# A 512-token block: other tokens on the 128 partitions, and its loads and stores cut into four pieces

## What is computed

```python
mod = (silu(c) @ w_ada + b_ada)                      # shift, scale, gate for both sub-layers
h = rmsnorm(x, norm1_g) * (1 + sc1) + sh1
u_in, gate_c, gate_b, q, k, v, g_conv, g_attn = split_projection(h @ w_in)
conv_y = short_conv(gate_c * u_in, conv_w, past)     # causal, width 3: needs tokens t-1 and t-2
y_conv = (gate_b * conv_y) @ w_conv_out
q, k = rope_partial(q, pos), rope_partial(k, pos)
attn_o = dilated_mixture(q, k, v)                    # 3 head groups, (window, dilation) = (128,1), (512,4), (2048,16)
mixed = (sigmoid(g_conv) * y_conv + sigmoid(g_attn) * (attn_o @ w_attn_out)) @ w_o
x = x + gt1 * mixed
x = x + gt2 * hier_moe(rmsnorm(x, norm2_g) * (1 + sc2) + sh2, ...)   # 16 experts, two per token
y = rmsnorm(x, normf_g)
# outputs: y, the keys and values of the prompt (k1_p ... v3_p; of group 1 only the last 128 tokens),
# the last two rows of the convolution's input, and the caches of the sampled sequences moved on by 4 rows
```

## Time and profile before

| | |
|---|---|
| median of three executions | 1200.55 us (1200.52 to 1203.01) |
| profiled execution: its own time | 1200.55 us |
| profiled execution: span from the first to the last instruction | 1198.5 us |
| PE busy | 94% of the span |
| DVE, ACT, POOL busy | 46%, 30%, 16% |
| mean granted clock of TensorE | 0.979 of full speed |
| bytes moved by DMA | 350.36 MB, mean 292 GB/s |

### The profile page before, as it was taken

One profiled execution on the slowest core, in us unless ns is written; L12 is line 12 of the kernel. 1 busy time (PEld: TensorE's weight loads), 2 busy tenths in 40 slices (PEclk: granted clock), 3 DMA queues, 4 the chain that ended last, 5 costly groups with the idle time before them and its releaser, 6 DMA issues.

```text
span 1198.5 us, 28853 instructions
## 1 busy us (share of the span) xinstructions
PE 1123.4 (94%) x12074; PEld 966.8 (81%) x12074; DVE 549.1 (46%) x1215; ACT 358.7 (30%) x655; POOL 187.0 (16%) x257
## 2 busy tenths in 40 slices
PE   4898999999999999999989999999969899999987
PEld 3797999999999998987769999999526567777762
DVE  1744565656565644543254444345723323322327
ACT  5422333333333323331054444432501101110103
POOL 0332233233330100000000000000050111111130
PEclk9998999999999999999979999999979999999998
DMA  9999978978756597748798788287729999999964
GB/s 351 387 342 374 328 253 296 315 240 284 279 185 219 184 376 270 264 158 298 269 335 301 264 290 297 88 275 294 287 75 356 376 411 419 408 403 409 420 170 143
DMA packets 167729, 350.36 MB, mean 292 GB/s; under 512 B 14670, under 2 KB 119326, under 8 KB 153105
## 3 DMA queue, kind: packets, MB, share of 16 engines
q1 hardware_dynamic: 151825, 324.91, 74.0%
q0 software_dynamic: 6272, 16.09, 4.4%
q10 hardware_dynamic: 9552, 8.21, 2.1%
HBM read 322.06 MB, written 115.20 MB: 365 GB/s over the span
## 4 chain that ended last, share of the span: by engine, by line
PE 85%; DVE 5%; DMA 4%; issue 3%; ACT 2%; SPq 1%; DVEq 0%; ACTq 0%
PE psum L927 44%; PE psum L1277 16%; PE psum L1289 7%; PE psum L1002 3%; PE psum L988 2%; PE psum L977 2%; PE psum L968 2%; PE psum L871 2%; PE psum L1024 2%; DMA kvr<-in_cache_v_dram 1%; DMA wraw<-in_w_in_dram 1%; DMA adar<-in_w_ada_dram 1%; PE psum L1051 1%; PE psum L1310 1%; PE psum L948 1%
## 5 line engine op out<-in xcount | busy, mean ns | idle before, releaser
L927 PE MATMUL psum<-hHi,whi 128*128 128x272 f32 x1216 | 359.0, 295 | 2.8 <-DVE hLo L1694 1.9
L927 PE MATMUL psum<-hLo,whi 128*128 128x272 f32 x1216 | 351.5, 289 | 0.0
L927 PE MATMUL psum<-hHi,wlo 128*128 128x272 f32 x1216 | 349.9, 288 | 0.0
L927 PEld LDWEIGHTS psum<-hHi,whi 128*128 128x128 f32 x1216 | 229.3, 189 | 15.6 <-issue 10.0
L927 PEld LDWEIGHTS psum<-hHi,wlo 128*128 128x128 f32 x1216 | 229.4, 189 | 0.0
L927 PEld LDWEIGHTS psum<-hLo,whi 128*128 128x128 f32 x1216 | 228.7, 188 | 0.0
L1277 PE MATMUL psum<-e,xs 128*32 128x256 f32 x3072 | 199.2, 384 | 22.3 <-issue 19.3
L1277 PEld LDWEIGHTS psum<-e,xs 128*32 128x32 f32 x3072 | 135.7, 111 | 80.9 <-issue 48.6
L1646 DVE TENSOR_TENSOR wlo<-wraw,whi 128x1024 fp32r<-128x1024 f32 x100 | 132.6, 1329 | 79.3 <-ACT whi L1382 78.5
L2399 POOL DMA_INDIRECT xg<-x_tok,piece x45 | 42.8, 952 | 463.2 <-DVE piece L2152 253.2
L1382 ACT ACTIVATE whi<-wraw 128x1024 fp32r<-128x1024 f32 x100 | 104.7, 1051 | 31.5 <-PE psum L927 24.8
(11 more groups left out here) (363 smaller groups left out, 1559.5 us busy)
## 6 DMA issues: line engine op xcount, KB each, us to landing
e<-in_w_dram SPq DMA_DIRECT2D x96, 1024.0 KB, 7.3
wraw<-in_w_in_dram SPq DMA_DIRECT2D x76, 512.0 KB, 6.0
out_dram<-in_cache_k_dram SPq DMA_DIRECT2D x32, 1022.0 KB, 9.3
out_dram<-in_cache_v_dram SPq DMA_DIRECT2D x32, 1022.0 KB, 8.0
adar<-in_w_ada_dram SPq DMA_DIRECT2D x36, 512.0 KB, 7.2
kvr<-in_cache_k_dram SPq DMA_DIRECT2D x8, 2048.0 KB, 9.8
kvr<-in_cache_v_dram SPq DMA_DIRECT2D x8, 2048.0 KB, 8.6
out_dram<-in_cache_k_dram SPq DMA_DIRECT2D x8, 1016.0 KB, 7.0
```

The source lines that it names most:

```text
L927: mm = pe.matmul(psum[:, t, 0:HALF], w[:, slot, k, :], x[:, k, cols], start=(k == 0 and n == 0), stop=(k == k_n - 1 and n == 2))
```

## The change

Column 128*a + 32*b + n now holds token 16*n + 4*b + a, with b from 0 to 3 and n from 0 to 31. A partition still has four neighbouring tokens, one in each tile, but the partition next to it has tokens 16 further on and not 4. A load or store with tokens on the partitions is issued as four DMAs, one for each b, with 32 partitions each (8 for the last 128 tokens of head group 1). Those are the two loads of `xt`, the two of `x2`, the 24 stores of keys and values and the four stores of y; the counts for which the semaphores are waited are four times as high. Each contiguous run in DRAM is as long as before. In `conv_prompt` the token before a token is found in two ranges of columns, so two of the three steps are split: five steps in place of three. The tables of masks and angles have other contents in the same shapes.

```diff
@@ -366,8 +366,9 @@
     w1_v = w1[0].rearrange("g e (p t) f -> (g e) p (t f)", t=XT)
     w3_v = w3[0].rearrange("g e (p t) f -> (g e) p (t f)", t=XT)
     w2_v = w2[0].rearrange("g e (p t) f -> (g e) p (t f)", t=FC)
-    xall_v = x_prompt[0].rearrange("(n a) d -> n a d", a=TILES)
-    yall_v = y_prompt[0].rearrange("(n a) d -> n a d", a=TILES)
+    xp_v = x_prompt[0].rearrange("(n b a) d -> a b n d", b=4, a=TILES)
+    yp_v = y_prompt[0].rearrange("(n b a) d -> a b n d", b=4, a=TILES)
+    xall_v = x_prompt[0].rearrange("(n b a) d -> b n a d", b=4, a=TILES)
     xs_v = x_sample.rearrange("b q d -> (b q) d")
     ys_v = y_sample.rearrange("b q d -> (b q) d")
 
@@ -694,8 +695,8 @@
                         sp.wait_ge(o_ev, UNITS * AC)
                         sp.wait_ge(qb_done, 3 * GROUPS * AC)
                         for k in range(2):
-                            sp.wait_ge(k_out[k], 16 * (GROUPS * AC // 2))
-                            sp.wait_ge(v_out[k], 16 * GROUPS * (AC // 2))
+                            sp.wait_ge(k_out[k], 64 * (GROUPS * AC // 2))
+                            sp.wait_ge(v_out[k], 64 * GROUPS * (AC // 2))
                     elif 2 <= w < K_UNITS + 2:
                         sp.wait_ge(ktr_pe, 2 * (dec_slots[unit_end(w - 2)][1] + 1))
                     elif w >= K_UNITS + 2:
@@ -766,7 +767,8 @@
 
                     sp.wait_ge(grp, 2 * (D0 - 1))
                     for a in (0, 2):
-                        sp.dma_start(x2[:, a:a + 2, :], xall_v[:, a:a + 2, :]).then_inc(xr_in, 16)
+                        for b in range(4):
+                            sp.dma_start(x2[32 * b:32 * b + 32, a:a + 2, :], xall_v[b][:, a:a + 2, :]).then_inc(xr_in, 16)
                 if m == D0 + RING + 1:
 
                     sp.wait_ge(g_lo, 2 * KC)
@@ -843,10 +845,11 @@
             for i, tt in enumerate(LAST_ORDER[1:] + LAST_ORDER[:1]):
                 sp.wait_ge(f_y, i + 1)
                 if tt < TILES:
-                    sp.dma_start(yall_v[:, tt, :], x2[:, tt, :]).then_inc(y_out, 16)
+                    for b in range(4):
+                        sp.dma_start(yp_v[tt, b], x2[32 * b:32 * b + 32, tt, :]).then_inc(y_out, 16)
                 else:
                     sp.dma_start(ys_v, x2[0:NS, tt, :]).then_inc(y_out, 16)
-            sp.wait_ge(y_out, 16 * (TILES + 1))
+            sp.wait_ge(y_out, 16 * (4 * TILES + 1))
             sp.wait_ge(shift_out, 16 * (SHIFTS_AB + 4 * KC))
             sp.wait_ge(state_out, 16 * (2 * GROUPS + 2))
             sp.wait_ge(new_out, 16 * GROUPS * (AC + 1))
@@ -1344,12 +1347,13 @@
         @block.scalar
         def _(act):
             for a in (0, 2):
-                act.dma_start(xt[:, a:a + 2, :], xall_v[:, a:a + 2, :]).then_inc(x_in, 16)
+                for b in range(4):
+                    act.dma_start(xt[32 * b:32 * b + 32, a:a + 2, :], xall_v[b][:, a:a + 2, :]).then_inc(x_in, 16)
             act.dma_start(xt[0:NS, TILES, :], xs_v).then_inc(x_in, 16)
             act.wait_ge(cst_in, 128)
             act.activation(ctok[:, :], ctok[:, :], ACT.Silu).then_inc(silu_done, 1)
             act.wait_ge(first_ev, 1)
-            act.wait_ge(x_in, 16 * 3)
+            act.wait_ge(x_in, 16 * 9)
             for tt in range(TILES + 1):
                 n = P if tt < TILES else NS
                 if tt:
@@ -1432,7 +1436,7 @@
                         act.wait_ge(vt_pe, n + 1)
                         if c >= 2:
                             act.wait_ge(pv_pe, UNITS * (c - 1))
-                            act.wait_ge(v_out[c % 2], 16 * GROUPS * (c // 2))
+                            act.wait_ge(v_out[c % 2], 64 * GROUPS * (c // 2))
                         act.activation(Vt[:, c % 2, :, g, :], psum[:, BANK_KV, :].rearrange("p (a n) -> p a n", n=P),
                                        ACT.Copy).then_inc(vt_ev, 1)
                 u = unit_at(G, 2)
@@ -1778,11 +1782,13 @@
                    .then_inc(cu_done, 1)
 
             def conv_prompt(tap):
-                tap(yv[:, 1:P], cu[:, 3 * P:SEQ - 1], 1)
+                tap(yv[:, 32:P], cu[:, 3 * P:SEQ - 32], 1)
+                tap(yv[:, 1:32], cu[:, SEQ - 32:SEQ - 1], 1)
                 tap(yv[:, 2 * P:SEQ], cu[:, 0:2 * P], 0)
                 y2 = yv[:, 0:2 * P].rearrange("p (a n) -> p a n", n=P)
                 c2 = cu[:, 2 * P:SEQ].rearrange("p (a n) -> p a n", n=P)
-                tap(y2[:, :, 1:P], c2[:, :, 0:P - 1], 0)
+                tap(y2[:, :, 32:P], c2[:, :, 0:P - 32], 0)
+                tap(y2[:, :, 1:32], c2[:, :, P - 32:P - 1], 0)
 
             def normalise(half):
 
@@ -1850,7 +1856,7 @@
                         dve.tensor_copy(Kns[P - NS:P, n % 2], psum[P - NS:P, BANK_MISC, 0:P]).then_inc(misc_ev, 1)
                         dve.wait_ge(kt_pe, n + 1)
                         if n >= 2:
-                            dve.wait_ge(k_out[n % 2], 16 * (n // 2))
+                            dve.wait_ge(k_out[n % 2], 64 * (n // 2))
                         dve.tensor_copy(Kst[:, n % 2].rearrange("p a n -> p (a n)"), psum[:, BANK_KV, :])\
                            .then_inc(kt_ev, 1)
                     else:
@@ -1964,7 +1970,7 @@
             def residual(f):
 
                 if f == 0:
-                    dve.wait_ge(xr_in, 16 * 3)
+                    dve.wait_ge(xr_in, 16 * 9)
                 dve.wait_ge(opT_pe, f + 1)
                 if f == 0:
                     own(dve.memset(sqp[:, :, :], 1.0))
@@ -2325,13 +2331,15 @@
             pool.wait_ge(ada_pe, len(ADA_FIRST))
             pool.memset(QB[:, :, :, :, :], 0.0).then_inc(zrow_done, 1)
             pool.wait_ge(zrow_done, 2)
-            prompt_v = [[prompt_kv[g][kv][0, 0].rearrange("(n a) h d -> n a (h d)", a=TILES)
+            prompt_v = [[prompt_kv[g][kv][0, 0].rearrange("(n b a) h d -> b n a (h d)", b=4, a=TILES)
                          for kv in range(2)] for g in range(GROUPS)]
 
             def store(g, kv, c, src, done):
 
-                lo = P - WINDOWS[0] // TILES if g == 0 else 0
-                pool.dma_start(prompt_v[g][kv][:, :, P * c:P * c + P], src[lo:P]).then_inc(done, 16)
+                lo = 24 if g == 0 else 0
+                for b in range(4):
+                    pool.dma_start(prompt_v[g][kv][b][:, :, P * c:P * c + P], src[32 * b + lo:32 * b + 32])\
+                        .then_inc(done, 16)
 
             rotated = 0
             for G in range(2 * B_P + 8):
@@ -2472,7 +2480,7 @@
     import numpy as np
 
     col = np.arange(SEQ)
-    time = TILES * (col % P) + col // P
+    time = 16 * (col % 32) + 4 * (col // 32 % 4) + col // P
     pos = np.concatenate([time, 2048 + np.arange(NS) % DEC_T]).astype(np.float32)
     freq = np.power(np.float32(500000.0), -np.arange(ROT, dtype=np.float32) / np.float32(ROT)).astype(np.float32)
     ang = (pos[:, None] * freq[None, :]).astype(np.float32).astype(np.float64)
```

## The result

| | before | after |
|---|---|---|
| median, measured together | 1202.28 us (5 runs, 1200.52 to 1203.49) | 1209.55 us (5 runs, 1205.86 to 1211.44) |
| ratio | | 1.0059, 95% interval 1.0036 to 1.0083 |
| the same kernels in a second comparison | 1195.9 us | 1204.36 us, ratio 1.0077 (1.0047 to 1.0107) |

The change makes the kernel 0.6% slower. The prediction was the same time (1201.8 us, range 1200.0 to 1204.2): both the size and the forecast of no change were wrong.

What follows compares the result with a forecast made beforehand. The prediction took PE, on the last-ending chain for 85% of the span, as the bound. To 1200.55 us it added 1.3 for the end and zero for all other terms: 1201.8 us, range 1200.0 to 1204.2.

Steps and rivals of the forecast that it cites:

- x2 in stage D: Stage D: six more issues move the w_o piece 2.8 us, covered by idle time; zero, or 0.5 us if late.
- The start: Kernel start: ACT issues 9 loads in place of 3, x arrives as before; zero, at worst ACT 1.56 us late.
- They stay full: Kernel start: the DMA engines stay full, so x is through at about 11.3 us, 1.1 before ACT's first square.
- the start slips: Rival, kernel start: the sampled tokens' small load lands late, x 1.56 us late, time 1203.4 us; chance 0.12.
- The end: Last stores of y: 16 issues at 0.445 us on SP put the last issue 1.28 us later (0.3 to 1.7).
- POOL and convolution: Stores of keys and values add 36 us to POOL, split convolution 3.8 us to DVE, both covered; zero.
- POOL as the bound of stage B: Rival, stage B: store pieces cost 0.952 us each, rotations come late by 8.5 us together, time 1210; chance 0.05.
- Rows further apart: Rival, kernel start: DRAM rows 64 KB apart halve the rate of x, time 1206 us; chance 0.06.

Runs made afterwards that it cites:

- the run across the middle: Kernel before with only x2's load cut into six pieces, partitions 32 to 95 first, then 0 to 31, then 96 to 127; x2 to `iota` 60.53 us.
- the strided pieces: Kernel before with only the x loads at the start cut into eight pieces, each taking every fourth partition; ratio 1.0017 (0.9994 to 1.004).
- the two queues: Kernel after with the pieces of xt, x2 and y for partitions 64 to 127 issued by POOL; ratio 1.0088 (1.006 to 1.0116).
- the complement: Kernel after with the old whole DMAs of x, x2 and y, so its output differs; against the kernel before, ratio 1.0 (0.9977 to 1.0023).

## Why the prediction was wrong

**"x2 in stage D: zero; 0.5 if the piece comes in late" failed.** This term was the largest miss: 4.6 us in the kernel after, 4.3 with this edit alone (63.24 less 58.99). The step counted what six more issues do to SP's queue. That was right as far as it went: the first piece of w_o behind x2 was issued 3.64 us after x2's first issue in place of 0.86, the 2.8 us that were predicted, and `tokt` was issued 8.4 us after it in both. What it left out is that the transfer itself takes longer. At 229 GB/s in place of 369 to 434 the 2 MB of x2 hold the engines some 4 us more (an estimate from these rates), and all that is queued behind them comes late: w_o for ACT, the rows of `tokt` (their issue took 2.96 us, where it was 0.34), and at last the sampled tokens' load, issued 13.05 us after x2's first issue in place of 10.20, for which DVE waits in `residual`. The runs with other splits of x2 bear this out. I looked for slack at ACT and SP. The tight place was DVE's wait for that small load, which stood in the trace of before with 4.0 us of idle time and which I did not read. A second thing was missing from the step: what PE loses after it has stood still. Its wait is 3.04 us, and the transposes and matmuls behind it take 1.59 us more at the lower clock, together the 4.63 us. Behind the wait of 1.1 us in the run across the middle the clock stayed at 1.00; behind waits of 2.5 to 3.4 us it fell to 0.50.

**"The start: I take zero" failed, and its bound was too low.** The first square came 2.5 us late. "They stay full" was right for the share and wrong for the rate. The rival that I called the start slips, the small load keeping its time from issue to landing, is what happened: it took 10.3 us in place of 9.6 from an issue 2.9 us later, where I had put the issue 2.7 us later. Its mechanism held, and its 1.56 us were 1.0 too few. How the slip divides between the later issue and the half rate is open: the strided pieces had more rate and a later issue, the two queues the half rate and an earlier one. How much of it reaches the end is not settled either: alone it gives 1.0022 (0.9996 to 1.0049).

**The end was right in mechanism and nearly in size.** 16 issues without a pause, 0.464 each where 0.445 was taken: 1.59 us in place of 1.28, the last issue 7.43 us after the first. Alone it gives 1.0017, with an interval that holds 1.

**POOL and convolution were right.** A piece takes 0.555 to 0.560 us (0.54 predicted), POOL has 35.6 us more (36), DVE 4.1 us (3.8), and no cost shows (0.9999, and 1.0 for the complement). POOL as the bound of stage B did not happen.

**Rows further apart: right rate, wrong cause.** This rival named the half rate, for the start alone, and had a chance of 0.06. The cause was in the same instruction, on the other side: which partitions it touches. The old rows with the cut loads are just as slow. That it named the right rate was luck.

The three places alone give 0.22, 0.42 and 0.17%, together 0.81%; cut together 0.72%, the kernel after 0.59 and 0.77%. Within their intervals these agree, and with 2.5 + 4.6 + 1.6 = 8.7 us, 0.7%. The mistake was one of kind: I priced a DMA cut in four by its issues, and took the bytes to flow as before, because the total of bytes was the same.

That the profiled execution of after is only 1.7 us longer in its span comes from two stretches that the change hardly touches. From the first projection matmul to the issue of x2 it took 739.4 us in it and 743.4 before, and from `iota` to the first store of y 345.75 and 350.06. In the other profiles the first of them lies between 738 and 745 us, with cut loads or without. The second lies between 345 and 350 us in the comparisons in which the kernel before takes 1196 to 1202 us (345.46 in the run across the middle, whose tokens are those of before), and between 307 and 310 us in those in which it takes 1157 and 1159: that is where the medians of the comparisons come to differ by 40 us. Neither cause was looked for. A single profile would have hidden the loss.

## What to carry to other kernels

When a DMA is cut or its view is changed, price three things apart: the issues, the partitions that each piece touches (both halves, or half the rate), and the outermost dimension (fewer than 16 there, fewer engines). A stretch in which the DMA share stays at 1 and the GB/s fall by half shows it at once. Look also for the smallest load at the end of the queue: at the start and in stage D of this kernel it was the one that others waited for. And where a late load makes PE stand still, look at the granted clock behind the wait; here a wait of 3.0 us cost 4.6.

## What the hardware showed that I had not expected

- All 16 engines busy, half the bytes: in stretches of 2 us, 32 neighbouring partitions or 64 of one half move 201 to 253 GB/s, 64 across the middle 336 and 352, 128 up to 434.
- A whole DMA with 4 blocks outermost ran on 4 engines at 61 to 76 GB/s; with 8 blocks 8 engines moved 111 and 119.
- The load of 128 KB behind the large ones at the start took 9.2 to 9.8 us from issue to landing where they went at full rate, 10.2 to 10.4 at half rate, and 8.4 behind the strided pieces, where it was issued last.
- The granted clock of TensorE fell to 0.50 (1.2 GHz) behind waits of PE of 2.5 to 3.4 us in stage D, and came back 3 to 5 us later; behind a wait of 1.1 us it stayed at 1.00.
- Stores issued by POOL as the last ones came in two profiles with a tail of 5 us and more in which nothing moves. Its cause stays open.
